# Moving the key and value stores, the convolution's LayerNorm and the wide queries in a two-layer decoder kernel, with a third value slot

## The reference: what is computed

```python
proj = h @ P['e_w_in'][e]
a_in = proj[..., :2 * A_CH]                       # A_CH = 256
qkv = proj[..., 2 * A_CH:].reshape(N, T, 3, B_GROUPS, B_HPG, B_HEAD_DIM)
glu = a_in[..., :A_CH] * jax.nn.sigmoid(a_in[..., A_CH:])
...
a = _causal_dwconv(a_ext, P['a_conv_w'][e], P['a_conv_b'][e])          # 31 taps
a = jax.nn.silu(_layernorm(a, P['a_ln_g'][e], P['a_ln_b'][e]))
for grp in range(B_GROUPS):                       # 4 heads of 64 each
    q, k, v = qkv[:, :, 0, grp], qkv[:, :, 1, grp], qkv[:, :, 2, grp]
    ...        # prompt: banded attention over dilated sub-sequences
    ...        # sample: 4 new tokens against a cache of keys and values
    kv_states.append(...)                         # keys and values are outputs too
alpha = jax.nn.softmax(jnp.stack(lses, axis=0), axis=0)
attn = jnp.sum(alpha[..., None] * jnp.stack(outs, axis=0), axis=0)
out = jnp.concatenate([a, attn], axis=-1) @ P['e_w_out'][e]
```

## Time and profile before

| | |
|---|---|
| median of 3 runs | 2751.89 us (2747.9 to 2755.22) |
| the profiled execution's own time | 2759.24 us |
| its span, first to last instruction | 2757.3 us |
| PE busy in the span | 2566.7 us (93%) |
| DVE, ACT, POOL busy | 961.0, 571.7, 529.4 us |
| mean granted TensorE clock | 0.959 of full speed |
| chain that ended last | PE 88%, DVE 6%, DMA 2%, ACT 1%, issue 1% |

### The profile page before, as it was taken

The page is one execution under the profiler, slowest core; times in us unless marked ns, Lnnn a source line. Parts: engine busy times, 40 slices in busy tenths (PEclk is TensorE's granted clock), DMA queues, the critical chain, the costliest instruction groups (busy, mean ns, idle before and its releaser), DMA issues.

```text
span 2757.3 us, 35559 instructions
## 1 busy us (share of the span) xinstructions
PE 2566.7 (93%) x16005; PEld 2429.7 (88%) x16005; DVE 961.0 (35%) x1508; ACT 571.7 (21%) x722; POOL 529.4 (19%) x175
## 2 busy tenths in 40 slices
PE   7898999697799999999999799998899999999996
PEld 4797777456799999999999799998799999999996
DVE  3454555234602222222222622337422222222226
ACT  3312222331411111111111411132311111111112
POOL 1321001101312211222212322211322222222220
PEclk8898999699899999999999899999899999999998
DMA  8112232355012222122222188511011111111101
GB/s 308 54 63 81 85 118 96 123 190 176 31 62 77 77 92 75 56 85 77 77 92 68 59 299 280 163 46 38 23 44 46 46 46 46 47 46 47 46 31 63
DMA packets 163522, 246.65 MB, mean 89 GB/s; under 512 B 5871, under 2 KB 150677, under 8 KB 162219
## 3 DMA queue, kind: packets, MB, share of 16 engines
q1 hardware_dynamic: 147358, 175.61, 19.2%
q0 software_dynamic: 3872, 60.82, 6.5%
q10 hardware_dynamic: 12140, 7.96, 1.0%
HBM read 225.69 MB, written 62.52 MB: 105 GB/s over the span
## 4 chain that ended last, share of the span: by engine, by line
PE 88%; DVE 6%; DMA 2%; ACT 1%; issue 1%; SPq 1%; ACTq 0%; DVEq 0%
PE ps L1818 75%; PE ps L1855 3%; PE ps L1929 2%; PE ps L2024 2%; PE ps L2042 1%; PE ps L1873 1%; DVE nt L1319 1%; DMA cache<-in_cache_b_kv 1%; PE ps L2074 1%; DMA scratch_o<-o_rows 1%; DVE conv_a L1374 1%; PE ps L1937 1%; PE ps L2033 1%; PE ps L1910 1%; PE ps L2063 1%
## 5 line engine op out<-in xcount | busy, mean ns | idle before, releaser
L1661 POOL TENSOR_TENSOR w_lo<-w_raw,w_hi 128x2048 fp32r<-128x2048 f32 x93 | 436.0, 4688 | 1798.1 <-ACT w_hi L864 1798.1
L1818 PE MATMUL ps<-h_hi,w_hi 128*128 128x352 f32 x3024 | 668.0, 329 | 6.1 <-DVE h_lo L1187 3.4
L1818 PE MATMUL ps<-h_hi,w_lo 128*128 128x352 f32 x3024 | 654.9, 324 | 0.0
L1818 PE MATMUL ps<-h_lo,w_hi 128*128 128x352 f32 x3024 | 654.7, 325 | 0.0
L1818 PEld LDWEIGHTS ps<-h_hi,w_hi 128*128 128x128 f32 x3024 | 512.7, 190 | 25.3 <-issue 20.7
L1818 PEld LDWEIGHTS ps<-h_hi,w_lo 128*128 128x128 f32 x3024 | 521.7, 189 | 0.0
L1818 PEld LDWEIGHTS ps<-h_lo,w_hi 128*128 128x128 f32 x3024 | 517.3, 189 | 0.0
L1180 DVE SCALAR_TENSOR_TENSOR x<-ps,mod,x 128x704 f32<-128x704 f32 x448 | 315.5, 746 | 320.5 <-PE ps L1818 320.5
L1227 DVE TENSOR_TENSOR tmp<-ps,tmp 128x1056 f32<-128x1056 f32 x44 | 55.3, 1258 | 729.7 <-PE ps L1818 729.7
L1818 PE MATMUL ps<-mid_hi,w_hi 128*128 128x352 f32 x1248 | 274.3, 328 | 10.0 <-DVE acc_s L1181 7.4
L864 ACT ACTIVATE w_hi<-w_raw 128x2048 fp32r<-128x2048 f32 x93 | 177.7, 1911 | 496.3 <-PE ps L1818 398.2
(11 more groups left out here) (258 smaller groups left out, 1736.5 us busy)
## 6 DMA issues: line engine op xcount, KB each, us to landing
w_raw<-in_ada_w SPq DMA_DIRECT2D x48, 1024.0 KB, 6.0
w_raw<-in_ffn_w_gate_up SPq DMA_DIRECT2D x44, 1024.0 KB, 5.2
out_kv_sample<-in_cache_b_kv POOLq DMA_DIRECT2D x8, 4088.0 KB, 18.9
w_raw<-in_ffn_w_down SPq DMA_DIRECT2D x22, 1024.0 KB, 5.0
cache<-in_cache_b_kv SPq DMA_DIRECT2D x32, 512.0 KB, 5.3
w_raw<-in_e_w_in SPq DMA_DIRECT2D x11, 1024.0 KB, 5.3
w_raw<-in_o_w_in SPq DMA_DIRECT2D x10, 1024.0 KB, 9.4
out_kv_sample<-in_cache_b_kv POOLq DMA_DIRECT2D x8, 1016.0 KB, 6.2
```

The source lines that it names most:

```text
L1661: pool.tensor_tensor(w_lo[raw_of[u].slot], w_raw[raw_of[u].slot], w_hi[u % 2].bitcast(F32), ALU.subtract)\
L1818: mm = pe.matmul(big(t)[:, b, 0:BLK], wt, xt[:, k, b * BLK:b * BLK + BLK], start=(k == 0 and n == 0), stop=(k == K - 1 and n == 2))
```

## The change

1. DMAs of `tokens_out` are issued by SP (`store_tokens`), not by ACT. SP walks a reordered list in which the store comes once SP has passed the 16 items that begin with `tokens_out`.
2. The taps are spread as 20, 30 and 12, the last 12 among v's pieces of the third group. `bias_in` of the third group and `ln_sum` stand behind the second of k's pieces, `ln_mean` between k and q, `ln_var` directly behind the third projection stage.
3. Copies to `mid_hi` and `mid_lo` leave `ln_var` and become an item of their own, `ln_mid`, in the merged part, after 12 of its attention items; `sample_load` stands behind it.
4. Only three items of `attention(2)` stand alone (`attend_qk` 0 and 1, `attend_tr` 0); `sample_in` with the wide queries comes after them, then the merged part with the other 61.
5. A third slot, `cache_v`, lies where the transposed keys were and is used for values alone. Its first load (sequence 2) is issued at `s_soft`, once the scores are done; each later load follows the product three before it. `o_sum`, which lay there, moves to the space of a value tile that is no longer needed, and its wait goes.

```diff
-    mixed(among(v + k + q, taps[0:14], 8), [])
+    mixed(among(v + k + q, taps[0:20], 8), [])
...
-    mixed(attention(0), among(among(v + k + q, taps[14:38]), [ada] * 8))
+    mixed(attention(0), among(among(v + k + q, taps[20:50]), [ada] * 8))
...
-    mixed(attention(1), among(among(v + k, taps[38:62]) + [one("bias_in", g=2)] + q[:2]
-                              + [lambda: items.append(Item("ln_sum", which="a", nt=2))] + q[2:], [ada] * 8))
-
+    k = k[:2] + [one("bias_in", g=2), norm_a[0]] + k[2:]
+    mixed(attention(1), among(among(v, taps[50:62]) + k + [norm_a[1]] + q, [ada] * 8))
     ada_out()
-    items.append(Item("ln_mean", which="a", nt=2, big=take("big")))
+    norm_a[2]()
+    last = attention(2)
+    mixed(last[:3], [])
     items.append(Item("sample_in"))
-    last = attention(2)
-    mixed(last[:8], [])
-    items.append(Item("ln_var", which="a", nt=2, big=take("big")))
-    items.append(Item("sample_load"))
...
-    half = (len(last) - 8) // 2
-    mixed(last[8:8 + half] + [one("x_back", k=1)] + last[8 + half:], sample)
+    half = (len(last) - 3) // 2
+    mixed(last[3:15] + [one("ln_mid"), one("sample_load")] + last[15:3 + half] + [one("x_back", k=1)] + last[3 + half:], sample)
...
+            def ahead():
+                out, done = [], 0
+                for i, it in enumerate(plan):
+                    if it.kind == "tokens_out":
+                        while done < min(i + 16, len(plan)):
+                            out.append(plan[done])
+                            done += 1
+                        out.append(Item("tokens_store", of=it))
+                return out + plan[done:]
...
+                elif it.kind == "tokens_store":
+                    store_tokens(it.of.g)
...
+                elif it.kind == "s_soft":
+                    load_cache(NB + 2)
+                elif it.kind == "s_pv" and it.b + 3 < NB:
+                    load_cache(NB + it.b + 3)
...
+                elif it.kind == "ln_mid":
+                    act.wait_ge(k_stored, 16 * K_STORES[1])
+                    act.wait_ge(ln_out, 2)
+                    for m in range(2):
+                        act.activation(mid_hi[:, 0, m, :], tmp[:, m, :], ACT.Copy).then_inc(mixed_hi, 1)
...
+                elif it.kind == "ln_mid":
+                    dve.wait_ge(k_stored, 16 * K_STORES[2])
+                    for m in range(2):
+                        dve.wait_ge(mixed_hi, m + 1)
+                        ins = low(mid_lo[:, 0, m, :], mid_hi[:, 0, m, :], tmp[:, m, :])
+                    ins.then_inc(mixed_ready, 1)
```

More of the change, by code:

```diff
@@ L733, in build_trunk, with cache_at, cached @@
         pt_item = next(it for it in plan if it.kind == "s_pt")
-        var_item = next(it for it in plan if it.kind == "ln_var" and it.which == "a")
+        def cache_at(c):
+            b = c - NB
+            return (c % 2, c // 2 + 1) if b < 0 else (b % 3, b // 3 + (1 if b % 3 == 2 else 5))
+        def cached(c):
+            slot = cache_at(c)[0]
+            return cache_v if slot == 2 else cache[:, slot]
         DOWN_M = (4, 5, 6, 7, 0, 1, 2, 3)
@@ L799, in load_cache @@
-                sp.dma_start(cache[:, c % 2, 5:9, :], rows[2].rearrange("(j s) e -> j s e", s=16)[:, 0:NS, :])\
-                    .then_inc(cache_loaded[c % 2], 16)
+                elif c == NB + 2:
+                    sp.wait_ge(big_ready, score_item.big + 1)
+                elif c > NB + 2 and b % 2:
+                    sp.wait_ge(v_used, (b - 3) // 2 + 1)
+                elif c > NB + 2:
+                    sp.wait_ge(misc_ready, values_of[b - 3].misc + 1)
+                rows = [A[f"cache_b_kv{g}"][0, b, :, kv].rearrange("w h e -> w (h e)") for g in range(3)]
@@ L813, in load_unit @@
                     load_raw(raw_of[u], as_down, w[256 * it.col:256 * it.col + 256, :].rearrange("(k p) n -> p k n", p=P))
-            for it in plan:
+            def ahead():
[7 more added lines that the diff above has]
+                return out + plan[done:]
+            for it in ahead():
                 if it.kind == "rel":
                     load_unit(0)
+                elif it.kind == "tokens_store":
+                    store_tokens(it.of.g)
                 elif it.kind == "ada":
@@ L1086, in _ @@
                     act.activation(q, q, ACT.Exp, scale=-0.5).then_inc(ln_rs, 1)
-                    if it.which == "a":
-                        act.wait_ge(k_stored, 16 * K_STORES[1])
                     for m in range(it.nt):
@@ L1095, in _ @@
                                            scale=vecs[:, G + m:G + m + 1]).then_inc(ln_out, 1)
-                            act.wait_ge(ln_out, m + 1)
-                            act.activation(mid_hi[:, 0, m, :], s if m == 0 else q, ACT.Copy).then_inc(mixed_hi, 1)
                         else:
@@ L1469, in _ @@
                         dve.tensor_tensor(v[:, m, :], v[:, m, :], q, ALU.mult).then_inc(ln_scaled, 1)
-                    if it.which == "a":
-                        dve.wait_ge(k_stored, 16 * K_STORES[2])
-                        for m in range(2):
-                            dve.wait_ge(mixed_hi, m + 1)
-                            ins = low(mid_lo[:, 0, m, :], mid_hi[:, 0, m, :], s if m == 0 else q)
-                        ins.then_inc(mixed_ready, 1)
+                elif it.kind == "ln_mid":
[4 more added lines that the diff above has]
+                    ins.then_inc(mixed_ready, 1)
                 elif it.kind == "down":
@@ L2112, in _ @@
                                        pT[:, t, b // 2:P:4],
-                                       cache[:, c % 2, t, :], start=(t < 4), stop=(t >= 5), skip_group_check=True)
+                                       cached(c)[:, t, :], start=(t < 4), stop=(t >= 5), skip_group_check=True)
                     mm.then_inc(misc_ready if b % 2 else v_used, 1)
```

70 lines of the change are left out of this document (33 added, 37 removed).

## The result

| | before | after |
|---|---|---|
| median | 2751.79 us (6 runs, 2747.9 to 2755.22) | 2732.32 us (6 runs, 2727.92 to 2742.55) |
| the profiled execution | 2759.24 us, span 2757.3 | 2729.51 us, span 2727.5 |
| ratio of the times | | 0.9928, interval 0.9911 to 0.9944 |

The change makes the kernel 19.5 us faster; 17.9 was forecast (2734), with a range of 2719 to 2748. The two profiled executions differ by more, 29.8 us of span, because the one of before was slower than each of its six timed runs (2755.22 at most) and the one of after the second fastest of its six.

The account below looks back on a forecast made before the run. PE, busy 93% of the span, bounds the kernel; time is won only where it idles or runs at low clock. Terms -17.6 - 3 + 1.5 + 1 + 4.2 - 4.8 + 0.5 = -18.2, carried to the median: 2734 us, range 2719 to 2748.

Parts of the forecast that it names:

- The first wait is ACT's DMA issues: Before the sample's scores: ACT's store issues delay q's second tile; with stores on SP, PE's 7.72 us wait goes.
- One chain of 14.4 us ended by an Exp on ACT: From the mean's start, LayerNorm steps up to the first softmax's Exp take 14.4 us, leaving PE one idle time.
- 9.5 us remain to be done after it: PE work left between chain and sample's first score matmul; 14.4 + 9.5 = 23.9 against 41.5, gain 17.6 us.
- The price of `ln_mid`: Merged part: its copies and subtractions among softmax steps cost 1.5 us of PE time (0 to 5).
- -3 for the low clock: After the shortened wait, PE's clock recovery falls on work already counted slow, so later work gains 3 us.
- The projection stages +4.2: Three projection stages: denser taps 0.5 and 3.2, third-stage relief -3, mean 2.0, `ln_mean` 1.5; 4.2 us slower.
- Values -4.8 + 0.5: Value products: third slot cuts cache waits, gaining 4.8 us; the later second output unit costs 0.5.
- Rival 3: Merged part: stores from SP land late behind cache loads, DVE stands at `ln_mid` some 8 us: 2742; chance 0.07.
- Rival 4: Before the scores: stores did not cause the first wait, q's tile stays late, 8 us remain: 2742; chance 0.07.
- Rival 5: The merged part stays at low clock, 50 us of matmuls becoming 85 or more: 2769, slower; chance 0.05.
- Rival 1: More comes back: projection stages 3 us faster, merged part keeps full clock once it has it: 2724; chance 0.15.
- Rival 2: DVE is the new bound: taps and `ln_mean` cost 12 us in the stages, `ln_mid` 5: 2745; chance 0.14.

Follow-up runs that it names:

- a_midend: The kernel after, with `ln_mid` and `sample_load` behind 39 instead of 12 attention items of the merged part, `x_back` ahead of them: 2724.74 us.
- b_taps: The kernel before with only the taps respread as 20/30/12, the last 12 among v's pieces: 2739.53 us, ratio 0.9952 to before.
- b_t14: The kernel before with only the taps respread as 14/36/12 instead of 14/24/24: 2749.03 us, ratio 0.9976 to before.
- b_t20: The kernel before with only the taps respread as 20/18/24 instead of 14/24/24: 2738.06 us, ratio 0.9939 to before.
- a_ln: The kernel after, with the stores issued by ACT again and two value slots instead of three: 2739.43 us, ratio 0.9945 to before.
- b_slot3: The kernel before with only the third value slot added: 2750.08 us, ratio 0.9986 to before.
- a_best: The kernel after, with LayerNorm scaling after 9 further attention items, and Silu, `ln_mid`'s copies and `sample_load` behind 39: 2719.61 us, ratio 0.9877 to before.

## Why the prediction was right

The forecast time was right and its mechanisms were mostly real, but two large terms were wrong in opposite directions, and that they cancelled to within 2 us is luck. Step by step:

- *The first wait is ACT's DMA issues: right.* q's evacuation starts at 490.73, as PE goes from q's last piece to the mean (490.89). Its price of 7.7 us holds only with the new chain; by itself it is 3.3.
- *One chain of 14.4 us ended by an Exp on ACT: right*, 13.1 us, one wait of 9.52. The 1.3 us less come mostly from Silu's table (1.28), which was not on the path.
- *"9.5 us remain to be done after it", and the merged part as long as before: wrong.* This is the step that failed. I counted the work in front of the sample's first score matmul and took everything behind it as unchanged but for 2.5 us of added items and 3 won by the clock. In front it came out shorter than forecast, 17.9 us (490.89 to 508.82) instead of 23.9. Behind it were 71.5 us in before (546.32 to 617.86) and are 85.7 in after (508.82 to 594.48), 5.2 of the 14.1 more as idle time and 8.9 as busy time of PE. The mean to the output projection gave 9.5 of 18.1. The price of `ln_mid` (1.5, bounds 0 to 5) and of the five items (1, bounds 0 to 3) was too low: a_midend's trace is 5.2 us shorter (103.59 to 98.41), but for the first together with the moved loads; for the second no run stands alone.
- *-3 for the low clock: wrong in sign.* After 9.52 us without work PE came back low just as before, and each of the three waits in the merged part brought a low spell of its own. Summed as above, the merged part stood at the low level for 14.7 of 71.5 us in before and for 32.7 of 85.7 in after: 18 us more, where I had expected fewer.
- *The projection stages +4.2: wrong in sign*, and the other large miss. Taps moved out of the third stage won 9 to 11 us there in the traces of b_taps and b_t14 (129.74 and 131.69 us) against before's 140.43, and still 4 to 6 against the shortest trace with all 24 (b_t20, 135.61), not 3; six more in the second cost nothing between 24 and 30. The mechanism was the one named (a tap held by a split, a late softmax step, a PE wait), but I priced the third stage's relief at one hold by the wait alone, and left out the clock that can fall behind it. The mean and `ln_mean` in the third stage cost 5.1 (a_ln against b_taps; 3.1 against b_t14), 3.5 was forecast.
- *Values -4.8 + 0.5: right in the sum*, 4.1 in runs; in b_slot3's trace its two terms were 8.3 and 2.6, so both were too small, and it is luck that they balanced.
- *Rival 3 (stores land late): not seen.* DVE never waited for `k_stored` at `ln_mid`, and SP issued the last store at 508.3, ahead of the next cache load at 515.73. *Rival 4: refuted* by the evacuation. *Rival 5 (the merged part stays at the low clock): seen in part.* 32.7 of its 85.7 us were low, in spells behind waits, and PE was back at 1.00 between them. *Rival 1* asked for stages 3 us faster and got 12 in the traces (the second and third), with nothing of what it asked of the merged part. *Rival 2 (DVE the new bound)* did not hold in the stages; in the merged part two of the three waits ended with DVE's copy of the keys.

The sum by runs: taps -13.8, stores -3.3, LayerNorm and queries -0.9, slot -4.1, -22.1 in all, against 19.5 for the whole change. The forecast by the same parts was +0.7, -7.7, -6.9 and -4.3: for the third, the -17.6 without the 7.7 of the first wait, and -3, +1.5, +1 and +3.5 with it. Each of the measured differences is uncertain by 3 to 5 us, and one that was measured on before need not hold on after.

## What to carry to other kernels

When a chain in front of a merged stretch gets shorter, count again what was hidden under it: softmax steps and copies that now have to be done inside the stretch come back as small waits, and what a shorter chain wins can be lost there. Price a wait of PE with the low clock that may stand behind it. And look at which instruction of one engine runs beside which of another, not at the mean load: here six taps moved from one stage to the one before it changed the time by more (16.1 us) than the whole restructuring of a LayerNorm (0.9). And where two edits are sized by one trace each, look first at how much of the difference lies where neither edit acts.

## What was not expected of the hardware

- The same 861 matmuls of a stage were busy for 139.17 us in before and for 130.62 in b_t20, with mean granted clocks of 0.92 and 0.99. In before a spell of 6.8 us at the lower of the two levels stood behind each of two waits of 3.60 and 2.20 us; behind one and the same wait of 1.38 us, at the head of the stage, it lasted 10.2 us in before and 3.4 in b_t20; and behind the waits of 1.70 and 1.78 us in b_t20's third stage there was none.
- A large tap (128x1024) is held by a split too: 3.27 to 4.58 us instead of 1.27 in the traces of b_taps, b_t20 and a_ln, and 2.16 for one begun near the split's end. The prediction had priced the small one only, though its rows 11 show one large tap of 3.27 us.
- ACT loaded the table of Silu at 496.83, 2.48 us before its input was ready at 499.31, so a switch in front of an awaited input cost nothing there. The Trainium skill (ScalarE: Activation LUTs, What ACT_TABLE_LOAD costs) adds a drain of about 1.38 us to each switch; in the trace of after the first Exp follows its table by 0.02 us (501.75 + 1.28 to 503.05), and in the earlier trace rows by 0.01.

Open is how much more a spread such as 32/18/12 would give on top of a_best: it joins the second stage of b_t20 and the third of b_taps, and was not run.
